# Two transformer blocks on 256 tokens: the last gate projection of the linear attention computed in two 64-row tiles

## The chip, the cores and the metric

The kernel runs on one NeuronCore of a Trainium2 chip. The metric is the device time of one execution in microseconds (us); lower is better. TensorE (PE) multiplies and writes to the eight banks of PSUM, each 128 partitions x 512 fp32; VectorE (DVE) and ScalarE (ACT) read PSUM and read and write the on-chip memory; GpSimd (POOL) does small vectors here; SyncE (SP) issues the loads.

## The reference, cut to what matters

Two blocks run one after the other on 256 tokens of width 1024. The second has dilated attention (24 heads in three groups), a gated linear attention (GLA, 4 heads with values of width 256), and a feed-forward part. The change touches one product of the second block, the projection `p_r`, whose Silu gates the output of the linear attention:

```python
h = rms_norm_2(x, norm1_g[l])
proj = jnp.einsum('bsd,de->bse', h, w_in[l])
p_attn, p_q, p_k, p_v, p_r, p_a, p_gate = jnp.split(proj, _IN_OFFSETS, axis=-1)
...
o_gla = rms_norm_2(o_gla, gla_out_norm_g[l]).reshape(b, s, GLA_DV) * jax.nn.silu(p_r)
```

`p_r` is 256 tokens x 1024; it is made as two chunks of 512 columns, and the change is on the second chunk alone.

## The kernel before

All products keep fp32 accuracy by splitting each operand into a high and a low part in the format fp32r (`h_hi`, `h_lo`, `w_hi`, `w_lo`) and adding three products: high x high, high x low, low x high. A weight slab of 1 MB lands in `raw` (three slots), issued by SP once the slot's earlier halves have been split. Each half slab then goes through ACT (`hi`, line 1218: the rounded high part) and DVE (`lo`, line 1715: the rest) into a ring of four half slabs. ACT may write ring entry n only when TensorE has finished half n - 4 (semaphore `mm_done`).

TensorE's work is one hand-written sequence. `chunk_rows` (lines 529 to 539) makes one chunk of 512 output columns for 256 tokens in four halves: for each of 8 slices of the contraction (128 rows each) and each of 2 token tiles, `half_rows` calls `passes` (lines 488 to 492), three matmuls of 128 rows x 128 columns of stationary operand and 512 moving columns. So a chunk is 8 x 2 x 3 = 48 matmuls. A chunk accumulates in the two banks of `pair(c)`: banks 0 and 1 for even c, 2 and 3 for odd c.

The loop at lines 1010 to 1016 (TensorE) runs t = 0 to 10. Chunks 0 to 8 are the attention's q, k and v, 9 and 10 are `p_r`. Between the halves of some chunks it turns attention heads through banks 6 and 7 (`turn_heads`) and makes one level of the linear attention's score matrix through banks 4 and 5 (`level`, lines 983 to 1008). Chunk t = 10 has neither; level 8 (t = 9) stands just ahead of it. Behind the loop, lines 1018 to 1027 make the output of the linear attention: for tokens a = 0 into banks 4 and 5 (line 1026), for a = 1 into banks 6 and 7 (lines 1025 and 1026). Then come gate projections as filler (`fill`, each part 6 matmuls of 256 columns) among the attention's scores (`att_score`, line 1066), turns of the weights (`att_turn`, line 368) and values (`att_value`, line 1096). `att_score(0)` waits for `acc_free0` to reach 14 (banks 0 and 1 read) and for `gla_go` to reach 2 (banks 4 to 7 copied out). It stands behind one `fill(4)`, 24 matmuls.

ACT's loop (lines 1549 to 1573) splits four halves per chunk, then empties the chunk from PSUM: `evacuate` (line 1232) waits for `mm_done` of the chunk's last half. For t = 9 and 10 the two activations are the Silu into `silu_r`, with the tokens' inverse root mean square as scale. After the loop come the two copies of the linear attention's output (line 1575, `go`), then the first exponential of the attention (line 1614).

DVE's loop (from line 2187) ends for t = 10 with `lo` of the two last halves; the last of these can only be cast by ACT when TensorE has finished the chunk, since the ring has four entries. After it DVE waits for the first attention scores (line 2257, masks). Much later (v = 3) DVE multiplies `go` by `silu_r`, after a wait for both chunks' evacuation. `asq` (128 x 1024 fp32) is the scratch of the heads' squares; nothing uses it at t = 10, and later `go_squares` lies on the same place.

Of the kernel before, what the change touches and what calls it, by code (L numbers as in the profile page):

```python
# [21 lines left out]
P = 128  # L22
# [3 lines left out]
ALU = mybir.AluOpType  # L26
ACT = mybir.ActivationFunctionType
# [3 lines left out]
TT = TOKENS // P  # L31
KT = D // P
EPS = 1e-6
RAW, RING = 3, 4
# [11 lines left out]
AH, AG, AD = 8, 3, 64  # L46
# [80 lines left out]
C_OUT, C_GLA, C_ATT, C_R = 9, 11, 16, 25  # L127
# [49 lines left out]
def ffn_columns(m):  # L177
# [28 lines left out]
    "gla_e gla_qe gla_level gla_taken gla_o gla_go gla_ssq gla_ready gate_free gate_done "  # L206
    "go_turned go_hi go_lo "

    "att_squared att_ms root_guessed root_found att_scaled att_turned att_T "
    "att_scores att_masked att_exp att_normed att_turnedp att_pt att_pv oa_hi oa_lo "  # L210
    "mix_taken mix_ready mix_hi mix_lo "

# [5 lines left out]
def two_blocks_kernel(nc, w, consts, out):  # L218
    with ExitStack() as ctx:
# [3 lines left out]
        bank = ctx.enter_context(nc.psum_tensor("bank", [P, 8, 512], F32))  # L223
        raw = sb("raw", [P, RAW, 2 * HALF])
        w_hi = sb("w_hi", [P, RING, HALF], F32R)
        w_lo = sb("w_lo", [P, RING, HALF], F32R)
# [7 lines left out]
        st = sb("stats", [P, 96])  # L234
        arena = sb("arena", [P, 26016])

        s = Semaphores(*[ctx.enter_context(nc.semaphore(n)) for n in SEMAPHORES])
        raw_in = [ctx.enter_context(nc.semaphore(f"raw_in{r}")) for r in range(RAW)]
        acc_free = (s.acc_free0, s.acc_free1)
# [6 lines left out]
        h_hi, h_lo = h_both[:, 0], h_both[:, 1]  # L246
# [31 lines left out]
        def pair(c, width=512):  # L278

            return bank[:, 2 * (c % 2):2 * (c % 2) + 2, 0:width]  # L280
# [63 lines left out]
        asq = area(23840, TT, 512)  # L344
# [3 lines left out]
        silu_r = area(0, TT, GH * GV)  # L348
# [138 lines left out]
        def _(pe):  # L487
# [41 lines left out]
            def chunk_rows(n, c, width, lhs, ready=None, halves=(0, 1, 2, 3), kn=2, free=None):  # L529

                if halves == LAST:
                    last_halves(n + 2, width, (4, 6), kn, lhs, [[(pair(c, width)[:, a], 0, width)] for a in range(TT)],
                                ready)
                    return
                for e in halves:
                    if e == 0:
                        pe.wait_ge(acc_free[c % 2], c // 2 if free is None else free)
                    half_rows(n + e, width, kn * e, kn, lhs, [[(pair(c, width)[:, a], 0, width)] for a in range(TT)],
                              e == 0, e == KT // kn - 1, ready)
# [74 lines left out]
            for a in range(TT):  # L614
                for k in range(2):
                    q = (10 + k) % RING
                    ins = passes(bank[:, 6, a * 256:(a + 1) * 256], a_hi[:, k, a * P:(a + 1) * P],
                                 a_lo[:, k, a * P:(a + 1) * P], w_hi[:, q, 512:768], w_lo[:, q, 512:768], k == 0, k == 1)
            ins.then_inc(s.uq_pe_done, 1)
            pe.wait_ge(s.acc_free1, 1)  # L620
            for j in range(MH // 2):
                for k in range(2):
                    q = (10 + k) % RING
                    ins = passes(bank[:, 2 + j // 2, j % 2 * TOKENS:(j % 2 + 1) * TOKENS], w_hi[:, q, j * P:(j + 1) * P],
                                 w_lo[:, q, j * P:(j + 1) * P], a_hi[:, k, :], a_lo[:, k, :], k == 0, k == 1)
            ins.then_inc(s.mm_done, 2)
            pe.wait_ge(s.lo_done, 13)
            for j in range(MH // 2):
                q = 12 % RING
                ins = passes(bank[:, 4 + j // 2, j % 2 * TOKENS:(j % 2 + 1) * TOKENS], w_hi[:, q, j * P:(j + 1) * P],  # L630
                             w_lo[:, q, j * P:(j + 1) * P], a_hi[:, 2, :], a_lo[:, 2, :], True, True)
# [11 lines left out]
            for a in range(TT):  # L643
                ins = turn(bank[:, 3, a * P:(a + 1) * P], k_pe[:, a, :])
# [338 lines left out]
            def level(t):  # L983
# [23 lines left out]
                                                       start=True, stop=True)  # L1007
                ins.then_inc(s.gla_level, 1)

            for t in range(3 * AG + 2):  # L1010
                chunk_rows(n2 + 18 + 4 * t, C_ATT + t, 512, h, halves=(0, 1))
                if 2 <= t < 3 * AG + 2 and (t - 2) % 3 < 2:
                    turn_heads(t - 2)
                chunk_rows(n2 + 18 + 4 * t, C_ATT + t, 512, h, halves=(2, 3))
                if 1 <= t <= 9:
                    level(t - 1)

            pe.wait_ge(s.gla_taken, 9)
            pe.wait_ge(s.att_T, 2 * AG)
            for a in range(TT):  # L1020
                for hd in range(GH):
                    o = bank[:, 4 + 2 * a + hd // 2, hd % 2 * GV:(hd % 2 + 1) * GV]
                    v = [gv[:, t, hd * GV:(hd + 1) * GV] for t in range(TT)]
                    if a == 1:
                        nc.tensor.matmul(o, g_cross[:, hd, :], v[0], start=True, stop=False)
                    ins = nc.tensor.matmul(o, g_in[:, hd, a, :], v[a], start=a == 0, stop=True)  # L1026
                ins.then_inc(s.gla_o, 1)
# [168 lines left out]
        def _(act):  # L1196
# [28 lines left out]
            def evacuate(dst, src, c, mm, func=ACT.Copy, rms=None):  # L1225

                act.wait_ge(s.mm_done, mm)
                if rms is None:
                    ins = nc.scalar.activation(dst, src, func)
                else:  # L1230
                    for a in range(TT):
                        ins = nc.scalar.activation(dst[:, a], src[:, a], func, scale=st[:, rms + a:rms + a + 1])
                ins.then_inc(acc_free[c % 2], 1)
# [315 lines left out]
            for t in range(3 * AG + 2):  # L1549
                n = n2 + 18 + 4 * t  # L1550
                hi(n + 4, n + 5)
                if 2 <= t < 3 * AG + 2 and (t - 2) % 3 < 2:
                    heads_out(t - 2)
                hi(n + 6, n + 7)
                g, part = t // 3, t % 3
                if t >= 3 * AG:
                    at = 512 * (t - 3 * AG)
                    evacuate(silu_r[:, :, at:at + 512], pair(C_ATT + t), C_ATT + t, n + 4, ACT.Silu, rms=8)
                else:
                    dst = av[:, :, g * 512:g * 512 + 512] if part == 2 else a_tok[:, part]  # L1560
                    evacuate(dst, pair(C_ATT + t), C_ATT + t, n + 4, rms=8)
                    if part < 2:
                        nth = 2 * g + part
                        c = C_ATT + t
                        act.wait_ge(acc_free[c % 2], c // 2 + 1)
                        if nth >= 1:
                            act.wait_ge(s.att_ms, nth)
                        nc.scalar.activation(asq, a_tok[:, part], ACT.Square, scale=AD ** -0.5).then_inc(
                            s.att_squared, 1)
                if t <= LEVELS:  # L1570
                    level_decay(t)
# [125 lines left out]
        def _(dve):  # L1697
# [541 lines left out]
            def gate_scaled(j):  # L2239
# [4 lines left out]
                                        r_row.rearrange("p (o t) -> p o t", o=1).to_broadcast([P, 2, TOKENS]),  # L2244
                                        ALU.mult).then_inc(s.gate_free, 1)

            dve.wait_ge(s.dil_in, 16)
            n = 2 * M_GATE + 4
            for v in range(AH):
                a = v // 4  # L2250
                keys = AG * (a + 1) * P
                dve.wait_ge(s.att_scores, v + 1)
                if v >= 1:
                    dve.wait_ge(s.att_turnedp, 2 * v if v <= 4 else AH + 4 * (v - 4))
                for e in range(2):
                    u = 2 * v + e
                    nc.vector.tensor_tensor_reduce(p[:, e, 0:keys], flat(bank[:, 4 * e:4 * e + 2, :])[:, 0:keys],
                                                   dil[:, 3 * P * a:3 * P * a + keys], 1.0, FAR, ALU.add, ALU.min,
                                                   st[:, 32 + u:33 + u]).then_inc(s.att_masked, 1)
                att_norm(2 * v)  # L2260
                att_norm(2 * v + 1)
                if v >= 1:
                    lo(n + 2 * v - 1)
                if v >= 5:
                    gate_scaled(v - 1)
                if v == 4:
                    out_lo(0)
                if v == 2:
                    dve.wait_ge(s.gla_ssq, 1)
                    root_guess(st[:, 16:24], st[:, 16:24], heads_newton[:, 0, 0:8], heads_newton[:, 1, 0:8]).then_inc(  # L2270
                        s.root_guessed, 1)
                if v == 3:
                    dve.wait_ge(s.root_found, 2 * AG + 1)
                    for c in (C_R, C_R + 1):
                        dve.wait_ge(acc_free[c % 2], c // 2 + 1)
                if 3 <= v < 7:
                    for at in (2 * v - 6, 2 * v - 5):
                        r, cols = at // GH, slice(at % GH * GV, at % GH * GV + GV)
                        ins = nc.vector.scalar_tensor_tensor(go[:, r, cols], go[:, r, cols], st[:, 16 + at:17 + at],
                                                             silu_r[:, r, cols], ALU.mult, ALU.mult)  # L2280
                    if v == 6:
                        ins.then_inc(s.gla_ready, 1)
                if v + 1 < AH:
                    lo(n + 2 * v)
                if v < 4:
                    gate_scaled(v)
# [113 lines left out]
```

## Time and profile before

| | us |
|---|---|
| median of 3 runs | 830.03 (830.02 to 830.12) |
| the profiled execution | 829.95 |
| its span, first to last instruction | 828.2 |

| engine | busy us | share of the span | instructions |
|---|---|---|---|
| PE (matmul) | 817.8 | 99% | 4918 |
| PEld (weight load) | 696.1 | 84% | 4918 |
| DVE | 592.5 | 72% | 912 |
| ACT | 471.8 | 57% | 698 |
| POOL | 40.2 | 5% | 88 |

The granted TensorE clock is 0.999 of full speed, and the DMA queues take about half of their engines' time. The duration of a matmul in the trace is from its start to its modelled end and is longer than its step in a dense sequence; the step is the difference between two starts. A row of the timeline that merges xN instructions gives the start of the first and the time until the end of the last.

### The profile page before, as it was taken

How to read it: one execution, taken by the hardware profiler on the slowest of the kernel's cores; microseconds unless marked ns; L12 is line 12 of the kernel's file. 1: busy time of each engine (PE TensorE's matmuls, PEld its weight loads, DVE VectorE, ACT ScalarE, POOL GpSimd, SP SyncE). 2: the span in 40 equal slices, each digit the busy share in tenths (PEclk: the TensorE clock that was granted, in tenths of full speed). 3: DMA queues.
4: the chain of work that ended last, by engine and by line, in shares of the span. 5: the costliest groups of instructions: out<-in, count | busy, mean ns of one | idle time of the engine just before them, and what ended most of it. 6: DMA issues, size and time to landing. Idle time of an engine off the chain costs nothing.

```text
span 828.2 us, 12685 instructions
## 1 busy us (share of the span) xinstructions
PE 817.8 (99%) x4918; PEld 696.1 (84%) x4918; DVE 592.5 (72%) x912; ACT 471.8 (57%) x698; POOL 40.2 (5%) x88
## 2 busy tenths in 40 slices
PE   9999999999999999999999999999999999999997
PEld 8877789888888887787888888888998888888886
DVE  6885589987777888567988963677577755566654
ACT  6676455665565566577565655565835644444441
POOL 0000000000000000002232400100000000000000
PEclk9999999999999999999999999999999999999999
DMA  9853244665556562835545453333456466555551
GB/s 331 287 178 133 63 142 154 203 204 181 175 200 195 169 250 83 305 109 197 178 157 175 154 188 116 102 104 102 134 179 196 154 203 203 185 179 192 173 183 51
DMA packets 89888, 142.14 MB, mean 172 GB/s; under 512 B 3681, under 2 KB 56289, under 8 KB 89713
## 3 DMA queue, kind: packets, MB, share of 16 engines
q1 hardware_dynamic: 89696, 141.37, 51.6%
q8 instruction: 32, 0.52, 0.3%
q10 hardware_dynamic: 144, 0.13, 0.1%
q14 instruction: 16, 0.12, 0.0%
HBM read 140.44 MB, written 1.05 MB: 171 GB/s over the span
## 4 chain that ended last, share of the span: by engine, by line
PE 88%; DVE 5%; ACT 4%; DMA 2%; issue 1%; SPq 0%; DVEq 0%; ACTq 0%
PE bank L490 19%; PE bank L491 18%; PE bank L492 18%; PE bank L563 15%; PE bank L565 8%; PE bank L368 3%; DVE w_lo L1715 2%; DMA raw<-in_w_in 2%; ACT w_hi L1218 1%; PE bank L1004 1%; PE bank L1096 1%; PE bank L1066 1%; PE bank L693 0%; PE bank L1026 0%; PE bank L717 0%
## 5 line engine op out<-in xcount | busy, mean ns | idle before, releaser
L1715 DVE TENSOR_TENSOR w_lo<-raw,w_hi 128x1024 fp32r<-128x1024 f32 (+2 forms) x260 | 307.0, 1203 | 80.0 <-ACT w_hi L1218 78.8
L1218 ACT CAST w_hi<-raw 128x1024 fp32r<-128x1024 f32 (+2 forms) x260 | 263.9, 1036 | 122.1 <-PE bank L492 113.7
L563 PE MATMUL bank<-a_both,w_hi 128*128 128x512 f32 x544 | 193.1, 398 | 0.0
L490 PE MATMUL bank<-w_hi,h_both 128*128 128x512 f32 (+1 forms) x480 | 190.4, 397 | 0.2 <-DVE w_lo L1715 0.2
L491 PE MATMUL bank<-w_lo,h_both 128*128 128x512 f32 (+1 forms) x480 | 186.6, 389 | 0.0
L492 PE MATMUL bank<-w_hi,h_both 128*128 128x512 f32 (+1 forms) x480 | 186.5, 388 | 0.0
L565 PE MATMUL bank<-a_both,w_lo 128*128 128x256 f32 x544 | 152.7, 281 | 0.0
L563 PEld LDWEIGHTS bank<-a_both,w_hi 128*128 128x128 f32 x544 | 102.2, 188 | 25.1
L490 PEld LDWEIGHTS bank<-w_hi,h_both 128*128 128x128 f32 x480 | 90.1, 188 | 20.6 <-issue 2.0
L492 PEld LDWEIGHTS bank<-w_hi,h_both 128*128 128x128 f32 x480 | 90.1, 188 | 18.6
L491 PEld LDWEIGHTS bank<-w_lo,h_both 128*128 128x128 f32 x480 | 90.2, 188 | 16.3
L565 PEld LDWEIGHTS bank<-a_both,w_lo 128*128 128x128 f32 x544 | 102.7, 189 | 0.9
L490 PE MATMUL bank<-h_both,w_hi 128*128 128x256 f32 (+1 forms) x200 | 60.0, 300 | 0.0
L491 PE MATMUL bank<-h_both,w_hi 128*128 128x256 f32 (+1 forms) x200 | 56.4, 282 | 0.0
L492 PE MATMUL bank<-h_both,w_lo 128*128 128x256 f32 (+1 forms) x200 | 56.4, 282 | 0.0
L2346 DVE TENSOR_TENSOR arena<-bank,arena 128x512 f32<-128x512 f32 x16 | 11.1, 691 | 56.1 <-ACT arena L1675 56.1
L490 PE MATMUL bank<-w_hi,a_both 128*128 128x512 f32 (+1 forms) x126 | 49.5, 393 | 0.3
L492 PE MATMUL bank<-w_hi,a_both 128*128 128x512 f32 (+1 forms) x126 | 48.8, 387 | 0.0
L491 PE MATMUL bank<-w_lo,a_both 128*128 128x512 f32 (+1 forms) x126 | 48.7, 387 | 0.0
L1675 ACT COPY arena<-bank 128x512 f32<-128x512 f32 x16 | 9.4, 587 | 65.8 <-PE bank L565 65.8
L490 PEld LDWEIGHTS bank<-h_both,w_hi 128*128 128x128 f32 (+1 forms) x200 | 37.3, 187 | 3.6 <-issue 2.7
L491 PEld LDWEIGHTS bank<-h_both,w_hi 128*128 128x128 f32 (+1 forms) x200 | 37.4, 187 | 0.3
(225 smaller groups left out, 1023.7 us busy)
## 6 DMA issues: line engine op xcount, KB each, us to landing
raw<-in_w_in SPq DMA_DIRECT2D x46, 1024.0 KB, 5.2
raw<-in_w_up SPq DMA_DIRECT2D x22, 1024.0 KB, 5.1
raw<-in_w_ff_up SPq DMA_DIRECT2D x16, 1024.0 KB, 5.5
raw<-in_w_ff_down SPq DMA_DIRECT2D x16, 1024.0 KB, 4.9
raw<-in_w_down SPq DMA_DIRECT2D x11, 1024.0 KB, 5.0
raw<-in_w_out SPq DMA_DIRECT2D x8, 1024.0 KB, 4.9
raw<-in_w_gla_branch SPq DMA_DIRECT2D x4, 1024.0 KB, 5.0
raw<-in_w_attn_branch SPq DMA_DIRECT2D x2, 1024.0 KB, 5.7
```

The costliest lines, as they stand in the source:

```text
L368: return nc.tensor.transpose(dst, src, ident[0:rows, 0:rows])
L490: nc.tensor.matmul(dst, l_hi, r_hi, start=start, stop=False)
L491: nc.tensor.matmul(dst, l_hi, r_lo, start=False, stop=False)
L492: return nc.tensor.matmul(dst, l_lo, r_hi, start=False, stop=stop)
L563: nc.tensor.matmul(acc.rearrange("p (o t) -> p o t", o=2), w_hi[:, q, k * P:(k + 1) * P], src[:, :, k, :], start=k == 0, stop=False)
L565: ins = nc.tensor.matmul(acc[:, 0:TOKENS], w_lo[:, q, k * P:(k + 1) * P], src[:, 0, k, :], start=False, stop=k == KT - 1)
L1004: ins = nc.tensor.matmul(bank[e * half:(e + 1) * half, 4 + hd // 2, at + e * half:at + (e + 1) * half], k_[:, hd, c:c + half], q_[:, hd, c ...
L1066: ins = nc.tensor.matmul(bank[:, 4 * e + at // 512, at % 512:at % 512 + keys], aqT[r:r + AD, k, a * P:(a + 1) * P], akT[r:r + AD, k, 0:key ...
L1218: nc.scalar.copy(dst, raw_half(m % RAW, half, size, cols)).then_inc(s.hi_done, 1)
L1675: nc.scalar.copy(up2[:, e, :].rearrange("p (f t) -> p f t", f=2), first_up(j)[:, :, TOKENS:2 * TOKENS]).then_inc(s.up_low, 1)
L1715: nc.vector.tensor_tensor(dst, raw_half(n // 2 % RAW, n % 2, size, cols), h, ALU.subtract).then_inc(s.lo_done, 1)
L2346: nc.vector.tensor_tensor(u, first_up(j)[:, :, 0:TOKENS], u, ALU.add).then_inc(s.up_summed, 1)
```

## The change

For t = 10 TensorE calls a new function, `row_tiles`, in place of `chunk_rows`. Each matmul of 128 contraction rows becomes two, of rows 0 to 63 and rows 64 to 127 (e = 0, 1), issued one behind the other: 96 matmuls in place of 48. Rows 0 to 63 accumulate in banks 0 and 1 as before, rows 64 to 127 in banks 6 and 7. Order of slices, tokens and passes, the waits on `lo_done` and the signals on `mm_done` stay. DVE, after its loop, copies banks 6 and 7 to `asq` and adds banks 0 and 1 to it; ACT's Silu reads `asq` in place of PSUM and waits for the sum. TensorE waits for the copy (`r_low`) ahead of the a = 1 part of the linear attention's output, which writes banks 6 and 7. `acc_free0` for banks 0 and 1 is now signalled by DVE's sum; the multiplication by `silu_r` waits for a semaphore of its own (`r_ready`).

```diff
+            def row_tiles(n, c):
+
+                pe.wait_ge(acc_free[c % 2], c // 2)
+                pe.wait_ge(s.att_T, 2 * AG)
+                for k in range(KT):
+                    q, at = (n + k // 2) % RING, k % 2 * 512
+                    pe.wait_ge(s.lo_done, n + k // 2 + 1)
+                    for a in range(TT):
+                        tok = slice(a * P, (a + 1) * P)
+                        for l_, r_, start, stop in ((h_hi, w_hi, k == 0, False), (h_hi, w_lo, False, False),
+                                                    (h_lo, w_hi, False, k == KT - 1)):
+                            for e in range(2):
+                                rows = slice(e * P // 2, (e + 1) * P // 2)
+                                acc = pair(c)[:, a] if e == 0 else bank[:, 6 + a, :]
+                                ins = nc.tensor.matmul(acc, l_[rows, k, tok], r_[rows, q, at:at + 512], start=start, stop=stop)
+                    if k % 2 == 1:
+                        ins.then_inc(s.mm_done, 1)
+
             for t in range(3 * AG + 2):
+                if t > 3 * AG:
+                    row_tiles(n2 + 18 + 4 * t, C_ATT + t)
+                    break
                 chunk_rows(n2 + 18 + 4 * t, C_ATT + t, 512, h, halves=(0, 1))
...
             for a in range(TT):
+                if a == 1:
+                    pe.wait_ge(s.r_low, 1)
                 for hd in range(GH):
...
-                    at = 512 * (t - 3 * AG)
-                    evacuate(silu_r[:, :, at:at + 512], pair(C_ATT + t), C_ATT + t, n + 4, ACT.Silu, rms=8)
+                    at, c = 512 * (t - 3 * AG), C_ATT + t
+                    if t == 3 * AG:
+                        evacuate(silu_r[:, :, at:at + 512], pair(c), c, n + 4, ACT.Silu, rms=8)
+                    else:
+                        act.wait_ge(acc_free[c % 2], c // 2 + 1)
+                        for a in range(TT):
+                            ins = nc.scalar.activation(silu_r[:, a, at:at + 512], asq[:, a], ACT.Silu, scale=st[:, 8 + a:9 + a])
+                        ins.then_inc(s.r_ready, 1)
...
+            c = C_ATT + 3 * AG + 1
+            dve.wait_ge(s.mm_done, n2 + 18 + 4 * (3 * AG + 1) + 4)
+            nc.vector.tensor_copy(asq, bank[:, 6:8, :]).then_inc(s.r_low, 1)
+            dve.wait_ge(s.r_low, 1)
+            nc.vector.tensor_tensor(asq, pair(c), asq, ALU.add).then_inc(acc_free[c % 2], 1)
             dve.wait_ge(s.dil_in, 16)
...
                     dve.wait_ge(s.root_found, 2 * AG + 1)
-                    for c in (C_R, C_R + 1):
-                        dve.wait_ge(acc_free[c % 2], c // 2 + 1)
+                    dve.wait_ge(acc_free[C_R % 2], C_R // 2 + 1)
+                    dve.wait_ge(s.r_ready, 1)
```

## Rows read from the trace of the kernel before

**Rows 1.** The page: busy time of each engine, granted clock, the chain by engine.
```profile
PE 817.8 (99%) x4918; PEld 696.1 (84%) x4918; DVE 592.5 (72%) x912; ACT 471.8 (57%) x698; POOL 40.2 (5%) x88
PEclk9999999999999999999999999999999999999999
...
PE 88%; DVE 5%; ACT 4%; DMA 2%; issue 1%; SPq 0%; DVEq 0%; ACTq 0%
```

**Rows 2.** Stages around the change, by windows: busy us, counts, clock, DMA share, GB/s.
```profile
core 0: us, PE busy (x) PEld busy (x) DVE busy (x) ACT busy (x) POOL busy (x), PEclk, DMA share, GB/s
...
492.00:503.10 11.10, 11.10 (x49) 9.20 (x50) 6.18 (x5) 5.69 (x6) 0.00 (x0) 1.00 0.46 141
503.10:511.00 7.90, 7.90 (x48) 7.20 (x47) 1.23 (x1) 5.41 (x6) 0.00 (x0) 1.00 0.61 200
511.00:583.00 72.00, 71.10 (x641) 64.17 (x640) 47.41 (x98) 41.95 (x90) 3.41 (x12) 1.00 0.31 99
```

**Rows 3.** Timeline of TensorE, start of chunk t = 10: start us, us, instruction.
```profile
490.04 0.39 PE L490 MATMUL bank<-w_hi,h_both 128*128 128x512 f32 x1
490.27 0.39 PE L491 MATMUL bank<-w_lo,h_both 128*128 128x512 f32 x1
490.50 0.39 PE L492 MATMUL bank<-w_hi,h_both 128*128 128x512 f32 x1
490.82 1.15 PE L1004 MATMUL bank<-arena 128*64 128x64 f32 x32
491.90 0.50 PE L490 MATMUL bank<-w_hi,h_both 128*128 128x512 f32 x1
492.23 0.39 PE L491 MATMUL bank<-w_lo,h_both 128*128 128x512 f32 x1
```

**Rows 4.** Timeline of TensorE, end of chunk t = 10 and the linear attention's output.
```profile
502.46 0.39 PE L491 MATMUL bank<-w_lo,h_both 128*128 128x512 f32 x1
502.68 0.40 PE L492 MATMUL bank<-w_hi,h_both 128*128 128x512 f32 x1
502.92 1.89 PE L1026 MATMUL bank<-arena 128*128 128x256 f32 x8
504.65 0.59 PE L1025 MATMUL bank<-arena 128*128 128x256 f32 x2
```

**Rows 5.** Timeline of TensorE, one 64-row group of attention scores; two windows of it.
```profile
551.64 0.70 PE L1066 MATMUL bank<-arena 64*128 64x256 f32 x4
551.64 1.57 PE L1066 MATMUL bank<-arena 64*128 64x256 f32 x12
```

**Rows 6.** Timeline of TensorE around the first attention scores.
```profile
510.73 0.28 PE L491 MATMUL bank<-h_both,w_hi 128*128 128x256 f32 x1
510.85 0.28 PE L492 MATMUL bank<-h_both,w_lo 128*128 128x256 f32 x1
511.06 0.94 PE L1066 MATMUL bank<-arena 64*128 64x128 f32 x12
511.93 0.39 PE L490 MATMUL bank<-h_both,w_hi 128*128 128x256 f32 x1
512.15 0.28 PE L491 MATMUL bank<-h_both,w_hi 128*128 128x256 f32 x1
```

**Rows 7.** Timeline of ACT and DVE between chunk t = 10 and the attention.
```profile
503.12 1.04 ACT L1218 CAST w_hi<-raw 128x1024 fp32r<-128x1024 f32 x1 [1.62 <-PE bank L492]
504.07 1.26 ACT L1232 ACTIVATE arena<-bank,stats 128x512 f32<-128x512 f32 x2
504.19 1.23 DVE L1715 TENSOR_TENSOR w_lo<-raw,w_hi 128x1024 fp32r<-128x1024 f32 x1 [1.44 <-ACT w_hi L1218]
505.22 1.01 ACT L1575 COPY arena<-bank 128x1024 f32<-128x1024 f32 x1
508.30 1.01 ACT L1575 COPY arena<-bank 128x1024 f32<-128x1024 f32 x1 [2.07 <-PE bank L1026]
509.33 1.28 ACT L1614 ACT_TABLE_LOAD   x1
512.15 0.56 DVE L2257 CUSTOM_DVE_ANT_0 arena<-bank,arena 128x384 f32<-128x384 f32 x1 [6.73 <-PE bank L1066]
```

**Rows 8.** The two instructions of line 1715 back to back, and the copy at line 2153.
```profile
479.79 2.35 DVE L1715 TENSOR_TENSOR w_lo<-raw,w_hi 128x1024 fp32r<-128x1024 f32 x2
L2153 DVE COPY arena<-bank x1: 1217/1217/1217, 355.9 to 355.9; 128x1024 f32<-128x1024 f32 x1
```

**Rows 9.** A wait of TensorE for DVE in the timeline: the end of DVE's work, the restart.
```profile
386.87 1.24 DVE L2193 TENSOR_TENSOR arena<-arena 128x1024 f32<-128x1024 f32 x1
388.16 0.19 PEld L992 LDWEIGHTS bank<-arena 128*128 128x128 f32 x1 [0.96 <-DVE arena L2193]
388.16 1.16 PE L992 MATMUL bank<-arena 128*128 128x128 f32 x8 [0.54 <-DVE arena L2193]
```

**Rows 10.** Timeline in the attention's first rounds: TensorE waits for ACT.
```profile
525.33 0.52 PE L368 MATMUL bank<-ident,arena 128*128 128x128 f32 x3 [0.78 <-ACT arena L1602]
```

**Rows 11.** The waits of the whole span: the longest one of TensorE.
```profile
PE bank L785 <- DVE arena L1875: 1.4, 1, 1.4
```

More of the change, by code:

```diff
@@ L207 @@
     "go_turned go_hi go_lo "
-    "att_squared att_ms root_guessed root_found att_scaled att_turned att_T "
+    "att_squared att_ms root_guessed root_found r_low r_ready att_scaled att_turned att_T "
     "att_scores att_masked att_exp att_normed att_turnedp att_pt att_pv oa_hi oa_lo "
```

## The prediction

> **What bounds the kernel now.** I read the page first: TensorE is busy for 99% of the span at a granted clock that never leaves full speed, and 88% of the chain that ended last is its own [rows 1]. So a saving or a stall of TensorE counts in full unless a later wait gives it back. Second, the busy time by stages: around the change (492 to 511 us) TensorE never rests, while ACT and DVE are busy for about half of it, and the DMA engines for 46 to 61% [rows 2]. Third, the timeline of the chunk that is changed. Its second matmul starts at 492.23 and its 48th at 502.68: 46 steps in 10.45 us, 0.227 us for 512 columns [rows 3, 4]. The recorded duration is 0.39, but the starts count. A weight load of 0.19 lies within each step (50 loads, 9.20 us busy, in a stage with TensorE at 100% [rows 2]), so loads are covered now. Last, ACT and DVE between chunk and attention, where the new work goes [rows 7]: ACT casts the last half slab at 503.12, as soon as the chunk is done; DVE splits it from 504.19 to 505.42 and then has nothing until 512.15, an idle time of 6.73 us.
>
> **The matmuls: 48 become 96.** Removed are 48 steps of 0.227 us, 10.9 us. Added are 48 pairs, and the question is what a pair costs. No row shows a 64-row matmul on fp32r operands. The nearest rows are the attention's scores: 64 rows by turns from both halves of the array into separate banks, on plain fp32, where each matmul is issued as two instructions. Four of them have ended after 0.70 us, twelve after 1.57: eight more, that is four pairs, in 0.87 us, 0.217 a pair [rows 5]. The same instruction shape on 128 rows, 256 columns of plain fp32, takes (504.65 - 502.92) / 8 = 0.216 each [rows 4]. So a pair of 64-row tiles costs exactly what one full matmul costs: they run side by side, and neither gains nor loses. Carried over, a pair of fp32r matmuls takes the 0.227 us of the full one: change 0. I take this value, since in the kind where both shapes are shown they are equal. The ends: at best the pair takes 0.216, the pace of plain fp32 over the same 512 array steps, and 48 x 0.011 = 0.5 us are gained; at worst the two don't overlap and 48 x 0.227 = 10.9 us are lost.
>
> The TensorE page of the Trainium skill, "TensorE: Matmul & The Clock Gate" (Part 3, The mechanism), says that a weight load overlaps running matmuls only when its row group differs; by this rule tiling would uncover time that full-array matmuls spend on loads. The trace disagrees that there is much to uncover: 0.19 of load and 0.39 of matmul fit into a step of 0.227.
>
> **The change of tile shape.** Going between full array and tiles costs some time: after the last full matmul at 510.85 the first tile starts at 511.06, 0.09 later than the 0.12 step, and on the way back the first step is 0.22 (511.93 to 512.15), 0.10 too long [rows 6]. With the first step inside the tiles and the late start of the way back, I put one crossing at about 0.19 us. Ahead of the chunk there is a crossing already: `level` runs in 64-column tiles, and the step behind it is 0.33 in place of 0.23 [rows 3]; it becomes another crossing of the same kind, cost 0 (at most 0.1). Behind the chunk there is a new one. It delays only the a = 0 part of the linear attention's output, and that is covered by the wait of the next part: cost 0, or 0.19 if that cover is gone.
>
> "TensorEngine Tiling (Array Packing)" of the Trainium skill (Key Properties) says that changing the tiling mode drains TensorE, and it recommends row tiles for a contraction of 64 or less. Both speak against this change, whose contraction is 128; the rows above agree with the drain.
>
> **The new wait of TensorE.** This is the term that I expect to decide. Part a = 1 writes banks 6 and 7, so it now waits until DVE has copied them. DVE reaches the copy only behind its split of the last half slab, which can't begin earlier: the cast waits for the end of the chunk. Times on the clock of before: the split starts at 504.19 [rows 7]; the following instruction starts 1.13 later (two take 2.35, one 1.22), at 505.32; a copy of 128 x 1024 out of PSUM took 1.217 us [rows 8], so the copy ends at 506.54. TensorE's load follows DVE's end by 0.05 (388.11 to 388.16), and the first step after such a rest is about 0.10 too long [rows 9]. So part a = 1, whose first instruction now starts at 504.65 [rows 4], effectively starts at 506.69: 2.04 us later. Part a = 0 ends at 504.81 and covers none of this further. Queued behind the waiting instruction on TensorE are the eight matmuls of a = 1, the gate filler and `att_score(0)`; the whole attention hangs on that one.
>
> **DVE's sum and the later Silu.** The sum starts at 506.59 and is as large as the split: 1.22, until 507.8. The Silu (1.26 for both tokens [rows 7]) moves from 504.07 to 507.9 and ends at 509.1; the first copy of `go` (1.01) ends at 510.1, and the second waits for the end of a = 1, 508.30 + 2.04 = 510.34, and ends at 511.35. `att_score(0)`, which needs both, comes at 511.06 + 2.04 = 513.10. These cost nothing: 1.75 us of gate filler hide them. If that cover were gone, every microsecond of it would be on the path. The ACT table load (1.28) then ends at 512.6, ahead of the first masks, which stand at 514.2. DVE's 2.4 us of copy and sum lie in its idle 6.73. The multiplication by `silu_r` is three attention rounds later. SP's loads are ordered by splits, of which none is moved, and no wait on a transfer appears from 503 us on.
>
> **Is the stall given back?** After `att_score(0)` ACT and DVE are in the same state as before, rested and waiting for it. In the first rounds TensorE does wait for ACT once, 0.78 us [rows 10], but the chain that it waits for started from the same scores and is as late. Nothing in 511 to 583 us has a due time of its own. I count nothing back.
>
> **Sum.** 0 (pairs) + 0 (crossings) + 2.04 (wait) = +2.04 us. Against the profiled execution, 829.95, that is 831.99; the median of the runs is 0.08 above the profiled one, so 832.1. A measurement of this kernel tells about 0.2%, 1.66 us, from no change; the forecast is just beyond.
>
> **Rivals.**
> 1. Row tiles are a bit faster than the full array on fp32r: the pair takes 0.216, as in plain fp32. For it: fp32r's step has 0.011 us that plain fp32 at the same 512 steps doesn't have, and separate row groups might hide it. Against it: plain fp32 shows both shapes equal, to 0.001. Price: 2.04 - 0.51 = +1.5, 831.6. This rival ends on the other side, not slower by the bound; it decides once a pair takes less than 0.227 - (2.04 - 1.66) / 48 = 0.219 us.
> By the rule on row groups cited above, 831.6 would be the result as well.
> 2. The tiles don't overlap on fp32r: both write a full column of PSUM in each array step, double what any row of this trace shows (the plain fp32 pairs need two steps a column). Price +10.9 + 2.0, 843; a partial conflict gives something between.
> 3. The stall is absorbed in the attention's first rounds, where TensorE has 0.78 us of wait: if ACT's casts and copies there are really set by something earlier, 0.8 of the 2.04 comes back, 831.3; more, up to all of it (830.0), if the following rounds give back too. Against: no such anchor is seen.
> 4. The clock falls during the rest. TensorE would rest from 504.8 to 506.6, 1.8 us; the longest rest of before is 1.4 us, at unchanged clock [rows 11, 1]. If it fell to 1.2 GHz, the stretch behind it would take double; a few microseconds of it are +2 to +4, 834 to 836.
> 5. The change gives a real gain: the a = 1 wait is short and pairs are quicker than 0.216. Nothing in the rows supports it.
>
> **How the numbers follow.** Forecast (832.0 to 832.4): 0.56. Rival 1 (831.4 to 831.7): 0.20. Rival 2: 0.08. Rival 3: 0.09, most of it within 0.2% of before. Rival 4: 0.04. Rival 5: 0.03. Range 831.0 to 833.4: it takes in the forecast with its bounds (+0.1 and +0.19 for the crossings, some tenths for hand-offs), rival 1, and the nearer half of rival 3; it leaves out rivals 2, 4 and 5. Faster: 0.03. Same: 0.20 + 0.06 = 0.26. Slower: 0.71.
>
> **What would show it.** In the profile of the changed kernel, the row matmuls start two within some nanoseconds, a pair each 0.227 us, and the chunk lasts 10.9 us; rival 1 shows 0.216 and 10.4, rival 2 up to 21.8. TensorE waits for DVE's copy for about 1.8 us ahead of line a = 1 and nowhere new else; the copy starts 1.1 us behind the split. `att_score(0)` is 2.0 us later against the end of the chunk, and so is everything to the end. The prediction is wrong if the pair step isn't 0.227, if the copy comes ahead of the split or lasts otherwise, or if the stretch from the first scores to the end is shorter than before.

## The result and the profile after

| | before | after |
|---|---|---|
| median of 10 runs, us | 830.01 (828.69 to 830.17) | 832.17 (830.71 to 832.62) |
| the profiled execution | 829.95 | 832.11 |
| its span | 828.2 | 830.3 |

The ratio is 1.0026, with a 95% interval of 1.0016 to 1.0036: 2.2 us slower, between 1.3 and 3.0. Both kernels have some executions about 1.2 us shorter than the rest; the one profile that caught such an execution (rows 0 to 63 only, below) has the last level 1.2 us earlier and everything from there on alike, so the stretches below are compared within one profile, from a fixed point on.

The page of the changed kernel, the same lines as [rows 1]:

```profile
PE 818.5 (99%) x4966; PEld 695.9 (84%) x4966; DVE 595.0 (72%) x914; ACT 472.1 (57%) x698; POOL 42.0 (5%) x88
...
PEclk9999999999999999999999999999999999999999
```

48 matmuls more, two DVE instructions more (2.5 us busy), and TensorE's busy time only 0.7 us up, though the span is 2.1 up: most of what was added is rest, not matmul time.

The timeline of TensorE from the last level to the first attention scores, to be laid beside [rows 3, 4, 6]:

```profile
490.90 1.15 PE L1004 MATMUL bank<-arena 128*64 128x64 f32 x32
491.98 0.50 PE L1024 MATMUL bank<-w_hi,h_both 64*128 64x512 f32 x2
492.32 0.39 PE L1024 MATMUL bank<-w_lo,h_both 64*128 64x512 f32 x2
492.55 0.62 PE L1024 MATMUL bank<-w_hi,h_both 64*128 64x512 f32 x4
...
502.77 0.39 PE L1024 MATMUL bank<-w_hi,h_both 64*128 64x512 f32 x2
503.09 1.99 PE L1049 MATMUL bank<-arena 128*128 128x256 f32 x8
506.69 0.70 PE L1048 MATMUL bank<-arena 128*128 128x256 f32 x2 [1.61 <-DVE arena L2278]
...
513.21 0.94 PE L1089 MATMUL bank<-arena 64*128 64x128 f32 x12
```

The reader is to see three things. First, the 64-row matmuls come in twos (x2, x4), and a row of two lasts no longer than one full matmul did, 0.39. From the first pair (491.98) to the last (502.77) are 10.79 us; in the kernel before the same stretch, 491.90 to 502.68, took 10.78 [rows 3, 4]. Second, part a = 0 starts 0.32 after the last pair, where it took 0.24 before, and its eight instructions take 1.99 in place of 1.89: the crossing. Third, part a = 1 starts 3.60 after a = 0, where it took 1.73. The bracket names DVE's copy.

The waits of TensorE over the whole span have one new entry, at the top; the 0.8 below it is the wait of [rows 10], unchanged:

```profile
PE bank L1048 <- DVE arena L2278: 1.6, 1, 1.6
PE bank L785 <- DVE arena L1904: 1.4, 1, 1.4
PE bank L601 <- DVE arena L1794: 1.2, 1, 1.2
PE bank L368 <- ACT arena L1631: 0.8, 1, 0.8
```

DVE and ACT between the chunk and the attention, beside [rows 7]:

```profile
504.28 1.23 DVE L1744 TENSOR_TENSOR w_lo<-raw,w_hi 128x1024 fp32r<-128x1024 f32 x1 [1.43 <-ACT w_hi L1241]
505.42 1.22 DVE L2278 COPY arena<-bank 128x1024 f32<-128x1024 f32 x1
506.67 1.22 DVE L2280 TENSOR_TENSOR arena<-bank,arena 128x1024 f32<-128x1024 f32 x1
...
507.93 1.33 ACT L1586 ACTIVATE arena<-arena,stats 128x512 f32<-128x512 f32 x2 [3.69 <-DVE arena L2280]
509.17 0.99 ACT L1604 COPY arena<-bank 128x1024 f32<-128x1024 f32 x1
510.45 1.02 ACT L1604 COPY arena<-bank 128x1024 f32<-128x1024 f32 x1 [0.29 <-PE bank L1049]
511.49 1.28 ACT L1643 ACT_TABLE_LOAD   x1
```

The copy begins 1.14 after the split begins and ends at 506.64; TensorE starts at 506.69. The Silu, 3.9 us later than before, is done early enough: both copies of `go` are out at 511.47, and TensorE reaches the scores at 513.21.

### The profile page after: what moved, and what is told of

Read it like the earlier page. It is cut to its first block, busy times and chain, and to the rows that moved or that the text cites. A ratio compares the mean times of both kernels' runs of the same rounds, so it can differ in the third digit from the quotient of the medians.

```text
span 830.3 us, 12783 instructions
## 1 busy us (share of the span) xinstructions
PE 818.5 (99%) x4966; PEld 695.9 (84%) x4966; DVE 595.0 (72%) x914; ACT 472.1 (57%) x698; POOL 42.0 (5%) x88
## 4 chain that ended last, share of the span: by engine, by line
PE 87%; DVE 5%; ACT 4%; DMA 3%; issue 1%; SPq 0%; DVEq 0%
PE bank L490 18%; PE bank L492 17%; PE bank L491 17%; PE bank L563 15%; PE bank L565 8%; PE bank L368 3%; DMA raw<-in_w_in 3%; DVE w_lo L1744 2%; ACT w_hi L1241 2%; PE bank L1024 1%; PE bank L1004 1%; PE bank L1119 1%; PE bank L1089 1%; PE bank L693 0%; PE bank L717 0%
## 5 line engine op out<-in xcount | busy, mean ns | idle before, releaser
L490 PE MATMUL bank<-w_hi,h_both 128*128 128x512 f32 (+1 forms) x464 | 184.1, 397 | 0.2 <-DVE w_lo L1744 0.2
L492 PE MATMUL bank<-w_hi,h_both 128*128 128x512 f32 (+1 forms) x464 | 180.3, 389 | 0.0
L491 PE MATMUL bank<-w_lo,h_both 128*128 128x512 f32 (+1 forms) x464 | 180.3, 389 | 0.0
L490 PEld LDWEIGHTS bank<-w_hi,h_both 128*128 128x128 f32 x464 | 87.1, 188 | 20.0 <-issue 2.0
L492 PEld LDWEIGHTS bank<-w_hi,h_both 128*128 128x128 f32 x464 | 87.1, 188 | 18.0
L491 PEld LDWEIGHTS bank<-w_lo,h_both 128*128 128x128 f32 x464 | 87.2, 188 | 15.8
L478 POOL TENSOR_TENSOR heads_newton<-heads_newton 128x16 f32<-128x16 f32 (+1 forms) x21 | 18.6, 884 | 492.8 <-DVE heads_newton L1751 491.7
L490 PEld LDWEIGHTS bank<-h_both,w_hi 128*128 128x128 f32 (+1 forms) x200 | 37.3, 187 | 3.6 <-issue 2.7
```

Source lines behind the costliest of these rows:

```text
L478: link(nc.gpsimd.tensor_tensor(t, y, y, ALU.mult))
L490: nc.tensor.matmul(dst, l_hi, r_hi, start=start, stop=False)
L491: nc.tensor.matmul(dst, l_hi, r_lo, start=False, stop=False)
L492: return nc.tensor.matmul(dst, l_lo, r_hi, start=False, stop=stop)
```

## The experiments

One measure serves all of them: the time in the profile from the first matmul of the last level (line 1004) to the first attention scores, and from there to the end of the span.

| kernel | level to scores | against before | scores to end | median of all runs |
|---|---|---|---|---|
| before | 20.24 | | 317.1 | 830.01 |
| changed kernel | 22.30 | +2.06 | 317.1 | 832.17 |
| copy first | 20.42 | +0.18 | 317.1 | 830.13 |
| wait only | 22.31 | +2.07 | 317.2 | 832.06 |
| copy twice | 23.44 | +3.19 | 317.1 | 833.63 |
| filler ahead of the wait | 20.87 | +0.63 | 317.1 | 830.57 |
| blocks of three | 22.33 | +2.09 | 317.1 | 832.08 |
| rows 0 to 63 only | 22.30 | +2.05 | 317.1 | 832.02 |
| blocks of six | 22.99 | +2.75 | 317.1 | 832.67 |
| blocks of twelve | 27.86 | +7.61 | 317.1 | 837.54 |

The fourth column is the same in all ten to 0.1 us: in these profiled executions nothing is lost and nothing is given back after the first scores. The ratios below are against executions of the kernel before that ran beside each variant; the medians of these were 829.86, 829.00 and 830.04, so a ratio can differ a little from what the last column gives. The stages of the table are the closer measure.

### The copy ahead of the split

```diff
-                lo(n + 6, n + 7)
+                lo(n + 6)
+                if t == 3 * AG + 1:
+                    dve.wait_ge(s.mm_done, n + 4)
+                    nc.vector.tensor_copy(asq, bank[:, 6:8, :]).then_inc(s.r_low, 1)
+                lo(n + 7)
...
-            dve.wait_ge(s.mm_done, n2 + 18 + 4 * (3 * AG + 1) + 4)
-            nc.vector.tensor_copy(asq, bank[:, 6:8, :]).then_inc(s.r_low, 1)
             dve.wait_ge(s.r_low, 1)
```

> The changed kernel with DVE's copy of banks 6 and 7 put ahead of its split of the last half slab; the sum stays behind the split. Theory A (all of the loss is TensorE's wait for a copy that stands behind the split): the copy starts when the chunk ends and is over 1.3 us later, before TensorE reaches part a = 1; only the crossing from tiles to the full array, 0.2 to 0.3 us, stays uncovered, and the time is 830.2 to 830.4. Rival B (the row tiles themselves, or the later Silu, cost part of it): a good part of the 2.1 us stays, 831 or more. Rival C (row tiles are faster and the wait hid it): below 830.0.

Measured: 830.13 (828.85 to 830.37), ratio 1.0002, interval 0.9993 to 1.0011. The rows of DVE and TensorE:

```profile
503.33 1.23 DVE L2232 COPY arena<-bank 128x1024 f32<-128x1024 f32 x1 [0.35 <-PE bank L1024]
504.47 1.22 DVE L1744 TENSOR_TENSOR w_lo<-raw,w_hi 128x1024 fp32r<-128x1024 f32 x1
505.60 1.22 DVE L2282 TENSOR_TENSOR arena<-bank,arena 128x1024 f32<-128x1024 f32 x1
```

```profile
503.21 1.99 PE L1049 MATMUL bank<-arena 128*128 128x256 f32 x8
505.04 0.59 PE L1048 MATMUL bank<-arena 128*128 128x256 f32 x2
```

The copy runs while ACT casts the last half slab, time in which DVE had nothing, and is over at 504.56. Part a = 1 follows a = 0 without a rest. Of the 2.06 us 1.88 are gone. The 0.18 that stay are the crossing behind the chunk, now with no wait over it. So the loss is a matter of one instruction's place in DVE's order, and theory A holds; rivals B and C fall. The median is just under the 830.2 to 830.4 that were expected, and the crossing, 0.18, just under its 0.2 to 0.3.

### The wait without the tiles

The edit is made in the kernel before; `chunk_rows` and the Silu out of PSUM stay.

```diff
+                if a == 1:
+                    pe.wait_ge(s.r_low, 1)
...
+            dve.wait_ge(s.mm_done, n2 + 18 + 4 * (3 * AG + 1) + 4)
+            nc.vector.tensor_copy(asq, bank[:, 6:8, :]).then_inc(s.r_low, 1)
             dve.wait_ge(s.dil_in, 16)
```

> The kernel before with full-array matmuls, and only the wait added: DVE copies banks 6 and 7 to the scratch behind its last split (the copy is used by nothing), and TensorE waits for it ahead of part a = 1. Theory A: the same loss as the whole change, +2.0 to +2.1 us, 832.1. Rival B: clearly less than the change, as the tiles' share and the Silu's are gone.

Measured: 832.06 (830.73 to 832.41), ratio 1.0028, interval 1.0018 to 1.0039, and +2.07 in the stage where the whole change has +2.06. TensorE:

```profile
502.94 1.89 PE L1028 MATMUL bank<-arena 128*128 128x256 f32 x8
506.64 0.70 PE L1027 MATMUL bank<-arena 128*128 128x256 f32 x2 [1.80 <-DVE arena L2250]
```

The wait is 1.80 here and 1.61 in the changed kernel; a = 1 starts equally long after the last level in both (15.80 and 15.79 us). The difference is the crossing, which the change hides under the wait. With full-array matmuls and the Silu in its old place the loss is the whole one, so neither tiles nor Silu are needed for it.

### A longer wait

```diff
             dve.wait_ge(s.mm_done, n2 + 18 + 4 * (3 * AG + 1) + 4)
+            nc.vector.tensor_copy(silu_r[:, :, 512:1024], bank[:, 6:8, :])
             nc.vector.tensor_copy(asq, bank[:, 6:8, :]).then_inc(s.r_low, 1)
```

> The changed kernel with the copy of banks 6 and 7 made twice, the first time into the place of the later Silu, so that TensorE's wait is 1.13 us longer. Theory A (a stall at this point reaches the end undiminished): +1.13 on the changed kernel, 833.3. Rival (part of the stall is given back in the attention's rounds): less than 0.9 more. Rival (the rest of TensorE, then 3.0 us, lowers its clock): over 1.5 more and a granted clock below 1.00 in the stage behind it.

Measured: 833.63 over 5 runs (833.04 to 834.96), ratio 1.0057, interval 1.0043 to 1.0071. In the profiled execution (833.35) the stage is +1.13 on the changed kernel (23.44 against 22.30, with rounding), and the stretch behind it is unchanged. The window rows (busy us and counts by engine, then clock) of the stage with the rest and of the attention:

```profile
503.10:513.00 9.90, 7.16 (x39) 6.09 (x38) 4.72 (x4) 4.56 (x6) 0.00 (x0) 1.00 0.51 166
513.00:586.00 73.00, 72.11 (x648) 65.08 (x647) 47.34 (x97) 42.55 (x90) 3.39 (x12) 1.00 0.30 95
```

TensorE rested for 2.74 us in the first of them, and the granted clock stays 1.00 in both. So theory A holds in this execution, and nothing is given back.

It is not the whole story of the five. Their times and mean granted clocks are 833.04 and 833.35 at 1.000, 833.63 and 834.96 at 0.998, and 834.82 at 0.997, while every other execution on record that has a clock beside it, of any kernel here, is at 0.999 or 1.000. By estimate, a mean of 0.998 or 0.997 is 3 to 5 us of the 833 at 1.2 GHz in place of 2.4; the kept traces have at most 2.3 us of that within the span, all of it behind the last matmul, where it costs nothing. So the last rival, a clock that falls after a rest this long, may have come true in two or three of the five executions, two of which took about 1.5 us more than the profiled one. No trace of such an execution was kept: where the clock fell, and that this rest was the cause, is not shown.

### Work put into the wait

```diff
                 if a == 1:
+                    fill(2)
                     pe.wait_ge(s.r_low, 1)
...
-            fill(4)
+            fill(2)
             att_score(0)
```

(`fill` is defined further up for this; nothing else differs.)

> The changed kernel with two of the four parts of gate filler (12 matmuls, 1.45 us) moved from behind part a = 1 to ahead of its wait. Theory A: TensorE's wait for the copy shrinks from 1.6 to about 0.2 us; the remaining two parts behind a = 1 (1.45 us) still cover the second copy of the linear attention's output (1.1 us); so 1.45 less than the changed kernel, 830.7. Rival (the first scores then wait for ACT's copies, which the later Silu holds up): less than 1 us is regained.

Measured: 830.57 (829.29 to 831.28), ratio 1.0007, interval 0.9998 to 1.0016; in the stage 1.43 less than the changed kernel. The wait is down to 0.19 (first row; the others are ACT's second copy of `go` and the scores):

```profile
506.80 0.70 PE L1071 MATMUL bank<-arena 128*128 128x256 f32 x2 [0.19 <-DVE arena L2279]
...
510.56 1.01 ACT L1605 COPY arena<-bank 128x1024 f32<-128x1024 f32 x1 [0.29 <-PE bank L1072]
511.88 0.94 PE L1090 MATMUL bank<-arena 64*128 64x128 f32 x12
```

The rival fails: the scores come at 511.88, ACT's second copy of `go` ended at 511.57. That cover is down to 0.3 us. A part is 0.72 us, so by estimate a third part moved ahead would have made the scores wait; that was not run.

### Blocks of three

```diff
-                        for l_, r_, start, stop in ((h_hi, w_hi, k == 0, False), (h_hi, w_lo, False, False),
-                                                    (h_lo, w_hi, False, k == KT - 1)):
-                            for e in range(2):
...
+                        for e in range(2):
...
+                            for l_, r_, start, stop in ((h_hi, w_hi, k == 0, False), (h_hi, w_lo, False, False),
+                                                        (h_lo, w_hi, False, k == KT - 1)):
```

> The changed kernel with another order in the chunk: the three passes of rows 0 to 63, then the three of rows 64 to 127, in place of turns. Theory A (matmuls start in program order; two run side by side only when neighbours in the order are of different row halves): six matmuls take 4 steps of 0.227 in place of 3, the chunk 64 steps, 14.5 us in place of 10.9, the time +3.6, 835.8. Rival (TensorE looks ahead and pairs them anyway): no change, 832.2. Rival (no overlap without turns): 96 steps, 21.8 us, +10.9.

Measured: 832.08 (830.89 to 832.42), ratio 1.0031, interval 1.0021 to 1.0041: no change against the turns. My theory A fell here and the rival held. The program now has the operands hi, lo, hi for rows 0 to 63 and then hi, lo, hi for rows 64 to 127; the trace, sorted by start, has them two by two:

```profile
492.27 0.50 PE L1024 MATMUL bank<-w_hi,h_both 64*128 64x512 f32 x2
492.60 0.40 PE L1024 MATMUL bank<-w_lo,h_both 64*128 64x512 f32 x2
```

Matmuls of different row halves start out of program order. The last two runs, with blocks of six and of twelve, test how far.

### Half of the rows

```diff
-                            for e in range(2):
+                            for e in (0,):
```

> The changed kernel without the matmuls of rows 64 to 127 of the chunk: half of that product is left out, 48 matmuls of 64 rows remain, and banks 6 and 7 hold what was in them. Theory A (a step depends on the 512 columns, not on the rows): each matmul still takes 0.227, the chunk 10.9 us, the time 832.2, no change. Rival (two tiles side by side slow each other): a step below 0.227, at best 0.216, and up to 0.5 us less.

Measured: 832.02 (830.72 to 832.41), ratio 1.0030, interval 1.0021 to 1.0040. One matmul of 64 rows after the other:

```profile
493.15 0.39 PE L1024 MATMUL bank<-w_lo,h_both 64*128 64x512 f32 x1
493.38 0.61 PE L1024 MATMUL bank<-w_hi,h_both 64*128 64x512 f32 x2
493.83 0.39 PE L1024 MATMUL bank<-w_lo,h_both 64*128 64x512 f32 x1
```

Three steps in 0.68, 0.227 each. Half the work takes as long as all of it (the chunk is 10.79 us from first to last start in both), and the second tile rides along for nothing. At 512 columns a matmul's step is 0.227 us, with 64 rows as with 128. It also explains why nothing was to be gained: a contraction of 128 filled the array already. The Trainium skill, "TensorE: Matmul & The Clock Gate" ("Why this matters for your kernels"), says the same of 32 rows, that one matmul takes as long as with 128 and the gain lies in tiles side by side; the trace agrees for 64.

### Blocks of six and of twelve

The loops over row halves go outside those over the token tiles (six), and outside those over both slices of a half slab f as well (twelve, with one wait on `lo_done` and one signal per half slab):

```diff
-                    for a in range(TT):
...
+                    for e in range(2):
...
+                        for a in range(TT):
```

```diff
+                    for e in range(2):
...
+                        for k in (2 * f, 2 * f + 1):
...
+                            for a in range(TT):
```

> The changed kernel with blocks of six in the chunk: for each slice of the contraction the six matmuls of rows 0 to 63 (two token tiles, three passes), then the six of rows 64 to 127. With blocks of three the trace had shown pairs although the program has none as neighbours. Theory D (TensorE starts matmuls of different row halves out of program order, and looks at least six matmuls ahead): pairs again, chunk 10.8 us, time as the changed kernel, 832.1. Rival (it looks only three ahead): between 3 and 6 matmuls of each block of twelve run alone, 9 steps in place of 6 or so, the chunk up to 16 us, +3 to +5 us.

> The changed kernel with blocks of twelve in the chunk: for each half slab the twelve matmuls of rows 0 to 63, then the twelve of rows 64 to 127. Theory D with a depth of twelve or more: pairs again, chunk 10.8 us, time 832.1. With a shorter depth d: the second row half starts about 12 - d steps late in the first block, and the pairs after it depend on how far TensorE may run ahead; the chunk is longer by up to 12 steps in each of 4 blocks, 10.9 us in all.

Measured: 832.67 (831.68 to 833.0) and 837.54 over 4 runs (836.5 to 838.06); ratios 1.003 (1.0018 to 1.0041) and 1.0088 (1.0071 to 1.0105). By the stage the chunk is 0.69 and 5.55 longer. The beginning of the chunk with blocks of six:

```profile
491.87 0.49 PE L1024 MATMUL bank<-w_hi,h_both 64*128 64x512 f32 x1
492.20 0.39 PE L1024 MATMUL bank<-w_lo,h_both 64*128 64x512 f32 x1
492.43 0.62 PE L1024 MATMUL bank<-w_hi,h_both 64*128 64x512 f32 x3
492.77 0.51 PE L1024 MATMUL bank<-w_lo,h_both 64*128 64x512 f32 x2
493.01 0.73 PE L1024 MATMUL bank<-w_hi,h_both 64*128 64x512 f32 x4
```

and with blocks of twelve:

```profile
491.78 0.49 PE L1026 MATMUL bank<-w_hi,h_both 64*128 64x512 f32 x1
492.12 0.39 PE L1026 MATMUL bank<-w_lo,h_both 64*128 64x512 f32 x1
492.35 0.62 PE L1026 MATMUL bank<-w_hi,h_both 64*128 64x512 f32 x2
492.81 0.39 PE L1026 MATMUL bank<-w_lo,h_both 64*128 64x512 f32 x1
493.05 0.62 PE L1026 MATMUL bank<-w_hi,h_both 64*128 64x512 f32 x2
493.50 0.39 PE L1026 MATMUL bank<-w_lo,h_both 64*128 64x512 f32 x1
493.73 0.61 PE L1026 MATMUL bank<-w_hi,h_both 64*128 64x512 f32 x3
494.07 0.50 PE L1026 MATMUL bank<-w_lo,h_both 64*128 64x512 f32 x2
```

Count the starts. With six, two matmuls start alone, and with the third (492.43) comes the first extra one: the seventh of the program. With twelve, eight matmuls start alone, 0.23 apart, and the extra one comes with the ninth (493.73): it is the thirteenth of the program. Both times a matmul of the other row half was started when it stood four places behind the one that starts beside it. The twelve repeat this: the 25th of the program starts beside the 21st (495.69), the 37th beside the 33rd (497.65).

The records don't name the row half, and the pairing follows from these counts. One record can be told for certain, the one that carries the signal of a half slab, its 24th matmul in the program. With blocks of six it starts at 495.08 and 25 matmuls have started before it, with blocks of twelve at 496.38 and 26 have: so at least two and three that stand behind it in the program started earlier.

From the third start on the six keep both halves busy, half a step apart, rows 0 to 63 in steps of 0.227 and rows 64 to 127 in steps of 0.231 until the two starts coincide. They lose three lone steps at the very end:

```profile
502.67 0.61 PE L1024 MATMUL bank<-w_hi,h_both 64*128 64x512 f32 x3
503.12 0.39 PE L1024 MATMUL bank<-w_lo,h_both 64*128 64x512 f32 x1
503.35 0.39 PE L1024 MATMUL bank<-w_hi,h_both 64*128 64x512 f32 x1
```

That is 3 x 0.227 = 0.68, the 0.69 measured. The twelve fall out of step in every half slab. So the depth is four in these runs. Theory D as it stood, at least six, is wrong, and so is its rival of three: for six the time came within 0.7 us of the first forecast although its condition fails, because the two halves need to fall out of step only once. For twelve the second forecast held, with d = 4: eight matmuls alone in the first block, and 5.55 us in all, within its 10.9. Whether the four are counted in matmuls, or as eight instructions with the weight loads, these runs can't tell apart.

## Why the prediction was right

The forecast was 832.1 with +2.04 us, at a chance of 0.56; the median is 832.17 and the stage has +2.06. The mechanism held too, as the copy put first and the wait without tiles show from both sides.

- **The pairs, 0.** Right: 10.79 us for the chunk against 10.78. The value was carried over from plain fp32 [rows 4, 5] by the argument that both shapes are equal there. No row of before showed a pair on fp32r, so this term was an argument and not a reading; the bounds given with it, +10.9 and -0.5 us, say how much hung on it. That two fp32r tiles each fill a PSUM column in every step, which rival 2 built on, does no harm.
- **The crossings, 0 net.** Right. The one ahead of the chunk has the same price as the one it replaces (0.33 step, both kernels). The one behind costs 0.18, seen bare in the run with the copy first, and is under the wait in the changed kernel. I had put it at 0.19. For the same reason TensorE's rest is 1.61 and not the 1.8 that I gave as a sign; without the tiles it is 1.80. The sum doesn't depend on it.
- **The wait, +2.04.** Right. The copy started 1.14 after the split (forecast 1.13), took 1.22, TensorE followed by 0.05, and its first two instructions lasted 0.11 longer than the same two in the kernel before (0.70 against 0.59).
- **Sum and Silu, 0.** Right: the copies of `go` ended 1.74 us ahead of the scores, forecast 1.75.
- **Given back, 0.** Right, and the profiled execution with the copy made twice shows it apart: 1.13 us more at that point are 1.13 us more at the scores, and the rest is the same.

Of the rivals, 1 needed a pair below 0.219 and found 0.227; 2 and 5 fall with the same rows; 3 falls with the stretch from the scores to the end; for 4 the clock stayed at full speed through the rest of 1.61 us, in the profile and by the mean (0.999 to 1.000) of all ten executions. With the rest of 2.74 us three executions of five have a lower mean clock; if that rest is the cause, which isn't shown, rival 4 was about a microsecond of rest away.

Two points of the working were not right though they cost nothing. I pictured the tiles as neighbours in the program that start together; the blocks of three show that this isn't needed. And "busy for about half" is true of DVE and ACT from 492 to 503 us only: from 503 to 511 DVE is busy for 1.23 of 7.90 us, 16%, and ACT for 68% [rows 2].

## What to carry to other kernels

When a new use of a buffer adds a wait, look where the instruction that frees the buffer stands in its own engine's order, and not only how long it takes: here a 1.2 us copy cost 2.06 us behind a split that itself waited for a cast, and nothing ahead of it, in time the engine spent idle. A longer stall may cost more than its length: with the rest at 2.74 us two executions of five took about 1.5 us more than the profiled one, at a lower mean clock; that the rest caused it is not shown. Two 64-row tiles take the time of one full matmul, and one 64-row tile alone takes as long as two; so row tiles can gain only where the contraction leaves rows of the array unused, and here they cost 0.18 us for the uncovered change of tile shape. No version here beats the kernel before; the best, with the copy first, is 0.18 us behind it in the stage, and the medians (830.13 against 829.86 beside it) don't tell the two apart.

## What the runs showed of the hardware that was not expected

TensorE started matmuls of different row halves out of program order. Each half kept a step of its own (0.227 us, 0.231 where the two were out of step), and a matmul was started beside one that stood up to four places ahead of it, not further (blocks of three: no loss; of six: 0.69 us; of twelve: 5.55 us for 96 matmuls). The Trainium skill's page "TensorE: Matmul & The Clock Gate" (Part 3, The mechanism) says that matmuls are strictly first in, first out and only weight loads are pulled ahead. These traces disagree, as far as the starts of matmuls in different row halves go; the measurement decides. Whether a signal can come before an earlier matmul of the program has ended was not tried: in all orders run here the signalling matmul was of the half that ran last within its half slab. What did happen is that matmuls behind the signalling one started before it. The ends in the trace are modelled and prove nothing here.
